# Three of the four quarters of the first modulations as fp32r pairs of high and low halves

## The chip, the cores and the metric

One core of one Trainium2 chip runs the whole program. The metric is the device time of one launch in microseconds. The engines work side by side, each through its own list of instructions in order, and wait for one another by semaphores: TensorE (PE in rows; its weight loads are PEld), VectorE (DVE), ScalarE (ACT), GpSimd (POOL) and SyncE (SP), whose list here is almost only DMA issues.

## The reference, cut to what matters

Two layers of a diffusion block over 512 latent and 256 context tokens of width 1024. What the change touches is the first sixth and second sixth of the adaLN modulations of layer 0 (shift and scale of the first norm), computed once for the latent and once for the context conditioning vector:

```python
silu_c = jax.nn.silu(c)
silu_ct = jax.nn.silu(c_ctx)
...
sh_a, sc_a, ga_a, sh_f, sc_f, ga_f = jnp.split((silu_c @ w_mod + b_mod)[:, None, :], 6, axis=-1)
tsh_a, tsc_a, tga_a, tsh_f, tsc_f, tga_f = jnp.split(silu_ct @ w_mod + b_mod, 6, axis=-1)
h = modulate(rms_norm(x, g_attn), sh_a, sc_a)
ht = modulate(rms_norm(xt, g_attn), tsh_a, tsc_a)
... = split_mixer_inputs(h @ w_in, qk_g)
... = split_mixer_inputs(ht @ w_in, qk_g)
```

`modulate(h, shift, scale)` is `h * (1 + scale) + shift`. All inputs are float32. Nothing of `h @ w_in` can begin before the shift and scale of its features are known.

## The kernel before

Activations lie features down, 128 features to a tile (`KT` = 8 tiles) and 768 tokens across (512 latent, 256 context). A product that must be near float32 is made of fp32r or f16 pairs: an operand is rounded to its high part, and the low part is the rest. `split` on GpSimd does it for a unit of weights (128 columns of `w_in`, in `raw_w`): one TENSOR_SCALAR writes the high half (L723) and one TENSOR_TENSOR subtracts it from the original for the low half (L726), into `split_w`. `dense_tile` (L958) then multiplies, for one feature tile k, weights high by activations high, weights low by activations high, and weights high by activations low: three products of 512 and 256 columns, six matmuls.

**The opening.** The first norm can't start without its modulations, and their weights, 8 MB for 2048 columns, come in four quarters, `mod_start[0..3]`: quarter i has the shift and the scale of feature tiles 2i and 2i+1. For each quarter:

1. TensorE, `first_modulations(i)` (L905): eight float32 matmuls, one for each input tile, with the two silu vectors (128x2) as weights and 512 columns moving, into the PSUM tile `small`.
2. ScalarE, `take_rows(i)` (L1385): the 2x512 result to `mod_rows`.
3. TensorE, `turn_first_modulations(i)` (L915): four transposes into `mod_ps`.
4. VectorE: `mod` = `mod_ps` plus bias (L1688), then `gain` from `mod` and the norm weights (L1692).
5. For each of the two tiles k: VectorE `scaled` = x_t times gain times inverse norm (L1773, its second tensor is `side` in PSUM), ScalarE `act` high = scaled plus shift, rounded (L1395, semaphore `h_hi`), VectorE `act` low = scaled plus shift minus high (L1757, function `lo`, semaphore `h_lo`). Each comes as two instructions, 512 and 256 columns.

TensorE takes the tiles in `dense_pair`: weight unit 0 at tile k and, `LAG` = 3 tiles later, unit 1. The next quarter's matmuls and transposes stand between tiles by hand:

```python
def in_tile(k):
    if l == 0 and k in (1, 3, 5):
        turn_first_modulations((k + 1) // 2)
    if l == 0 and k in (2, 4):
        first_modulations(1 + k // 2)
    pe.wait_ge(h_hi, 2 * l * KT + k + 1)
```

Quarter 1's eight matmuls come ahead of tile 0. GpSimd has nothing between the split of unit 1 and that of unit 2, which waits until unit 0's matmuls are done, since both use one slot of `split_w`. SyncE issues, in this order: tokens, mod_start 0 and 1, weight units 0 and 1, mod_start 2, small constants, mod_start 3. Everything behind the opening (units 2 to 15, attention, output projection, FFN, second layer) is the same in both kernels.

## Time and profile before

| | |
|---|---|
| median of 3 runs | 1706.69 us (1705.18 to 1708.16) |
| the profiled execution, its own time | 1705.99 us |
| its span | 1704.2 us |
| TensorE busy | 1632.2 us (96%) |
| VectorE, ScalarE, GpSimd busy | 1025.6, 745.2, 739.6 us |

The span is from the first to the last instruction; the time has 1.8 us more around it. Busy time of an engine says how much of the span it had an instruction in flight. The chain that ended last follows, back from the end, at each step what released the waiting instruction; "issue" is a step for which the profile shows no wait. A time in brackets behind a row of the timeline is what the engine idled before it, and for whom.

### The profile page before, as it was taken

Reading aid. Unit: us, or ns where it says so; the run is one execution under the profiler, and the core shown is the slowest. Engines: PE = TensorE matmul, PEld = TensorE weight load, DVE = VectorE, ACT = ScalarE, POOL = GpSimd, SP = SyncE. Lnnn points to the kernel's source line nnn. Section 1 sums busy time; section 2 is a strip of 40 time slices with the busy share of each in tenths; the row PEclk is TensorE's granted clock in tenths of the full one; section 3 lists DMA queues with packets and bytes.
Section 4 is the critical chain, followed back from the end, with each engine's and each line's share of the span. In section 5 each row is a group of like instructions: output and inputs, shape, how many; then the busy total and the mean of one; then the engine's idle time right before and its main releaser. Section 6 shows DMA issues by size and latency. Waiting matters only on the chain.

```text
span 1704.2 us, 29725 instructions
## 1 busy us (share of the span) xinstructions
PE 1632.2 (96%) x11685; PEld 1120.3 (66%) x11685; DVE 1025.6 (60%) x2075; ACT 745.2 (44%) x1367; POOL 739.6 (43%) x474
## 2 busy tenths in 40 slices
PE   7999989998999999999999999997998899999998
PEld 3688878977856656666666667886887544444444
DVE  3434498884479873788358855456995526326234
ACT  4222278884144341334313323225894455355342
POOL 1244335572614443344433343550403567567563
PEclk9999999999989999999999999998999899999999
DMA  9355453323045412353326232554103242243222
GB/s 325 58 133 138 118 150 98 94 63 88 26 123 161 137 56 93 99 164 120 113 75 225 79 69 53 135 135 114 28 6 101 62 136 87 75 136 96 66 87 87
DMA packets 317290, 179.24 MB, mean 105 GB/s; under 512 B 88527, under 2 KB 310495, under 8 KB 317151
## 3 DMA queue, kind: packets, MB, share of 16 engines
q1 hardware_dynamic: 284542, 143.63, 30.6%
q10 hardware_dynamic: 32608, 33.71, 6.2%
q8 instruction: 93, 1.52, 0.4%
q14 instruction: 47, 0.38, 0.1%
HBM read 158.97 MB, written 2.83 MB: 95 GB/s over the span
## 4 chain that ended last, share of the span: by engine, by line
PE 73%; DVE 15%; issue 5%; ACT 3%; DMA 2%; SPq 1%; POOL 1%; ACTq 0%; DVEq 0%; POOLq 0%
PE acc L958 60%; DVE mod_acc L2148 4%; DVE prob L1930 2%; DVE prob_t L1936 2%; PE small L905 2%; PE mod_ps L1058 1%; PE side L1143 1%; PE side L895 1%; ACT prob_t L1516 1%; PE acc L1126 1%; PE acc L1127 1%; DVE mod_acc L2146 1%; ACT prob L1494 1%; DMA tokens<-in_ctx 1%; PE mod_ps L1143 1%
## 5 line engine op out<-in xcount | busy, mean ns | idle before, releaser
L958 PE MATMUL acc<-act,pair_w 128*128 128x512 f16 x3168 | 580.2, 345 | 5.6 <-ACT act L1395 3.5
L958 PEld LDWEIGHTS acc<-act,pair_w 128*128 128x128 f16 x3168 | 309.5, 99 | 265.5 <-issue 10.6
L958 PE MATMUL acc<-act,split_w 128*128 128x512 f32 (+1 forms) x1920 | 378.6, 355 | 9.3 <-DVE act L2080 4.6
L958 PEld LDWEIGHTS acc<-act,split_w 128*128 128x128 f32 x1920 | 307.7, 189 | 63.6 <-DVE act L2080 6.8
L799 POOL TENSOR_SCALAR pair_raw<-pair_raw,weight_scale 128x1024 f32<-128x1024 f32 x88 | 109.6, 1246 | 324.9 <-ACT pair_w L1566 324.9
L958 PE MATMUL acc<-hidden,down_w 128*128 128x512 f16 (+1 forms) x1056 | 247.8, 343 | 1.6 <-DVE hidden L2114 0.8
L723 POOL TENSOR_SCALAR split_w<-raw_w 128x1024 fp32r<-128x1024 f32 x72 | 77.1, 1071 | 342.9 <-PE acc L958 231.0
L2148 DVE SCALAR_TENSOR_TENSOR mod_acc<-mod_chunk,silu_c,mod_acc 128x256 f32<-128x256 f32 x280 | 198.0, 751 | 4.0
L802 POOL TENSOR_TENSOR pair_w<-pair_raw,pair_w 128x1024 f16<-128x1024 f32 x88 | 192.4, 2187 | 7.3
L726 POOL TENSOR_TENSOR split_w<-raw_w,split_w 128x1024 fp32r<-128x1024 f32 x72 | 171.9, 2388 | 6.0
L2109 DVE SCALAR_TENSOR_TENSOR prod<-acc,prod_scale,silu_g 128x768 f32<-128x768 f32 (+1 forms) x44 | 38.9, 884 | 208.0 <-PE acc L958 199.0
L958 PEld LDWEIGHTS acc<-hidden,down_w 128*128 128x128 f16 x1056 | 100.5, 98 | 85.2 <-POOL down_w L818 2.8
L958 PE MATMUL acc<-hidden,down_low 128*128 128x512 f16 (+1 forms) x528 | 152.6, 343 | 0.0
L1635 ACT ACTIVATE hidden<-prod 128x768 f16<-128x768 f32 (+1 forms) x44 | 32.4, 736 | 238.4 <-DVE prod L2109 238.4
L1494 ACT ACTIVATE prob<-prob,stat 128x768 f32<-128x768 f32 (+5 forms) x160 | 121.7, 761 | 32.7 <-DVE prob L1930 25.8
L1930 DVE TENSOR_SCALAR_CACHE_REDUCE prob<-acc,score_scale 128x768 f32<-128x768 f32 (+4 forms) x128 | 102.7, 802 | 12.0 <-PE acc L1127 9.2
L1566 ACT ACTIVATE pair_w<-pair_raw,weight_scale 128x1024 f16<-128x1024 f32 x88 | 95.9, 1137 | 16.5 <-DVE weight_scale L2027 16.5
L1555 ACT ACTIVATE squares_out<-pair_raw 128x1024 bf16<-128x1024 f32 x88 | 92.4, 1050 | 7.5 <-DMA pair_raw<-in_w_up 3.5
L1784 DVE SCALAR_TENSOR_TENSOR x_t<-acc,down_gate,x_t 128x512 f32<-128x512 f32 x72 | 45.4, 658 | 80.4 <-PE acc L958 80.2
L1628 ACT ACTIVATE silu_g<-acc,weight_scale 128x768 f32<-128x768 f32 (+1 forms) x44 | 34.6, 786 | 132.9 <-PE acc L958 99.5
L1126 PE MATMUL acc<-ks,qs 128*128 128x256 f16 (+1 forms) x384 | 91.6, 270 | 0.0
L1127 PE MATMUL acc<-ks,qs 128*128 128x256 f16 (+1 forms) x384 | 89.3, 269 | 0.0
(229 smaller groups left out, 2462.8 us busy)
## 6 DMA issues: line engine op xcount, KB each, us to landing
mod_chunk<-in_w_mod ACTq DMA_DIRECT2D x28, 1024.0 KB, 5.2
pair_raw<-in_w_gate SPq DMA_DIRECT2D x44, 512.0 KB, 3.7
pair_raw<-in_w_up SPq DMA_DIRECT2D x44, 512.0 KB, 4.8
raw_w<-in_w_in SPq DMA_DIRECT2D x64, 256.0 KB, 3.8
raw_w<-in_w_mod SPq DMA_DIRECT2D x24, 512.0 KB, 4.0
raw_w<-in_w_down SPq DMA_DIRECT2D x20, 512.0 KB, 4.5
mod_start<-in_w_mod SPq DMA_DIRECT2D x8, 1024.0 KB, 11.0
ks<-q_split SPq DMA_DIRECT2D x64, 96.0 KB, 2.4
```

Of the source, the lines that this page charges most:

```text
L723: pool.tensor_scalar(split_w[slot][:, 0, 0:n, :], raw_w[slot][:, 0:n, :], 1.0, 0.0, ALU.mult, ALU.add).then_inc(hi_w, 1)
L726: pool.tensor_tensor(split_w[slot][:, 1, 0:n, :], raw_w[slot][:, 0:n, :], split_w[slot][:, 0, 0:n, :].bitcast(F32), ALU.subtract).then_inc ...
L799: pool.tensor_scalar(raw, raw, weight_scale[:, 1, 2 * f + s:2 * f + s + 1], 0.0, ALU.mult, ALU.add).then_inc(weight_mul, 1)
L802: pool.tensor_tensor(w[:, s, 1, :, :], raw, w[:, s, 0, :, :], ALU.subtract).then_inc(pair_ready, 1)
L958: mm = pe.matmul(acc[slot][:, a:b], own, moving[:, part == 1, k, a:b], start=(k == 0 and part == 0), stop=(k == n - 1 and part == 1))
L1126: pe.matmul(out_, q, ks[:, s["k"], 0, k0:k0 + size], start=True, stop=False)
L1127: mm = pe.matmul(out_, q, ks[:, s["k"], 1, k0:k0 + size], start=False, stop=not masks)
L1494: sc.activation(p, p, ACT.Exp, bias=stat[:, 1, i:i + 1], scale=-1.0, accum_out=stat[:, 2, i:i + 1]).then_inc(exps, 1)
L1555: sc.activation(squares_out[:, :], pair_raw[home(f)][:, s, :, :].rearrange("p k n -> p (k n)"), ACT.Square, accum_out=weight_sum[:, 2 * f ...
L1566: sc.activation(pair_w[home(f)][:, s, 0, :, :], pair_raw[home(f)][:, s, :, :], ACT.Copy, scale=weight_scale[:, 1, 2 * f + s:2 * f + s + 1] ...
L1930: ve.tensor_scalar(out_, src, minus, None, ALU.mult, ALU.min, accum_out=lowest).then_inc(scored, 1)
L2148: s = ve.scalar_tensor_tensor(**kw, in1=kw["out"], op0=ALU.mult, op1=ALU.add)
```

## The change

Quarter 0 stays as it is. Quarters 1 to 3 are taken as pairs. ScalarE rounds `mod_start[i]` to fp32r in four pieces of 128x1024 (`round_first`, into `mod_high`), and GpSimd, or VectorE for the first `LOW_BY_DVE[i]` pieces, subtracts them for the low halves (`split_first` and `low_first`, in place, as `mod_low`). TensorE runs eight fp32r matmuls on the high halves and eight on the low ones, with the four columns of `silu4` (high and low of both vectors) as weights, and the result has four rows. The transposes of these quarters become small matmuls with `fold`, which also adds the rows of the high and the low silu. TensorE's order in the first pair of units changes too: unit 1 follows unit 0 tile by tile, with no lag. SyncE loads weight unit 0 ahead of mod_start 1.

```diff
+LOW_BY_DVE = [0, 2, 0, 0]
...
             load_start(0)
+            load_in(0, 0)
             load_start(1)
-            load_in(0, 0)
             load_in(0, 1)
             load_start(2)
...
+                def split_first(i):
+
+                    pool.wait_ge(mod_start_in[i], 32)
+                    for p in range(LOW_BY_DVE[i], 4):
+                        pool.wait_ge(first_hi, 4 * (i - 1) + p + 1)
+                        pool.tensor_tensor(mod_low[i][:, 2 * p:2 * p + 2, :], mod_start[i][:, 2 * p:2 * p + 2, :],
+                                           high_at(i, 2 * p, 2).bitcast(F32), ALU.subtract).then_inc(first_lo_pool, 1)
+
                 for j in range(16):
                     split(u_in(l) + j, 8)
+                    if l == 0 and j == 1:
+                        for i in range(1, N_START):
+                            split_first(i)
...
+            def high_modulations(i):
+
+                pe.wait_ge(mod_rows_ready, i)
...
+                for k in range(KT):
+                    if k % 2 == 0:
+                        pe.wait_ge(first_hi, 4 * (i - 1) + k // 2 + 1)
+                    pe.matmul(small[0:4, :], silu4[:, k, :], high_at(i, k, 1).rearrange("p k n -> p (k n)"),
+                              start=(k == 0), stop=False)
+
+            def low_modulations(i):
+
+                for k in range(KT):
+                    if k == 0 and sum(LOW_BY_DVE[:i + 1]):
+                        pe.wait_ge(first_lo_dve, sum(LOW_BY_DVE[:i + 1]))
+                    if k == 2 * LOW_BY_DVE[i]:
+                        pe.wait_ge(first_lo_pool, 4 * i - sum(LOW_BY_DVE[:i + 1]))
+                    mm = pe.matmul(small[0:4, :], silu4[:, k, :], mod_low[i][:, k, :], start=False, stop=(k == KT - 1))
                 mm.then_inc(mod_start_done, 1)
...
+                def first_pair(r):
+
+                    for k in range(KT):
+                        in_tile(k)
+                        dense_tile(0, split_w[0], k, KT, act, TOK, in_tile_low)
+                        if k == 0:
+                            pe.wait_ge(split_ready, r + 2)
+                        if k % 2 and k < KT - 1:
+                            low_modulations((k + 1) // 2)
+                        dense_tile(1, split_w[1], k, KT, act, TOK)
+                        if k % 2 and k < KT - 1:
+                            turn_first_modulations((k + 1) // 2)
+                            if k < KT - 3:
+                                high_modulations((k + 3) // 2)
...
+            def round_first(i, pieces):
+                sc.wait_ge(mod_start_in[i], 32)
...
+                for p in pieces:
+                    sc.activation(high_at(i, 2 * p, 2), mod_start[i][:, 2 * p:2 * p + 2, :], ACT.Copy).then_inc(first_hi, 1)
...
-                    if nu == 0 and k % 2 == 0:
+                    if nu == 0 and k == 0:
+                        round_first(1, (0, 1))
+                        take_rows(0)
+                        round_first(1, (2, 3))
+                    elif nu == 0 and k % 2 == 0:
+                        if k < KT - 2:
+                            round_first(k // 2 + 1, range(4))
                         take_rows(k // 2)
...
+                def low_first(i):
+
+                    for p in range(LOW_BY_DVE[i]):
+                        ve.wait_ge(first_hi, 4 * (i - 1) + p + 1)
+                        ve.tensor_tensor(mod_low[i][:, 2 * p:2 * p + 2, :], mod_start[i][:, 2 * p:2 * p + 2, :],
+                                         high_at(i, 2 * p, 2).bitcast(F32), ALU.subtract).then_inc(first_lo_dve, 1)
+
...
+                    if nu == 0 and k % 2 and k < KT - 1:
+                        low_first((k + 1) // 2)
```

GpSimd's list at the start, before. The numbers behind a tile's name tell its buffers apart (`split_w_52` and `_53` are the slots of units 0 and 1, and then of units 2 and 3).

```order
L723 TENSOR_SCALAR split_w_52<-raw_w_50 128x1024
L726 TENSOR_TENSOR split_w_52<-raw_w_50,split_w_52 128x1024
L723 TENSOR_SCALAR split_w_53<-raw_w_51 128x1024
L726 TENSOR_TENSOR split_w_53<-raw_w_51,split_w_53 128x1024
L723 TENSOR_SCALAR split_w_52<-raw_w_50 128x1024
L726 TENSOR_TENSOR split_w_52<-raw_w_50,split_w_52 128x1024
```

The same place now (L733 and L736 are the split, L756 is `split_first`):

```order
L733 TENSOR_SCALAR split_w_52<-raw_w_50 128x1024
L736 TENSOR_TENSOR split_w_52<-raw_w_50,split_w_52 128x1024
L733 TENSOR_SCALAR split_w_53<-raw_w_51 128x1024
L736 TENSOR_TENSOR split_w_53<-raw_w_51,split_w_53 128x1024
L756 TENSOR_TENSOR mod_low_124<-mod_start_121,mod_high_128 128x1024 x2
L756 TENSOR_TENSOR mod_low_125<-mod_start_122,mod_high_129 128x1024 x2
L756 TENSOR_TENSOR mod_low_125<-mod_start_122,mod_high_130 128x1024 x2
L756 TENSOR_TENSOR mod_low_126<-mod_start_123,mod_high_131 128x1024 x2
L756 TENSOR_TENSOR mod_low_126<-mod_start_123,mod_high_132 128x1024 x2
L733 TENSOR_SCALAR split_w_52<-raw_w_50 128x1024
L736 TENSOR_TENSOR split_w_52<-raw_w_50,split_w_52 128x1024
```

Ten two-input subtractions now stand between the split of unit 1 and that of unit 2. VectorE's list from the first modulations of quarter 0 to those of quarter 1, before:

```order
L1688 TENSOR_TENSOR mod<-mod_ps,vecs 128x2x4
L1692 SCALAR_TENSOR_TENSOR gain<-mod,vecs 128x4
L1773 SCALAR_TENSOR_TENSOR scaled_137<-x_t,gain,side 128x512
L1773 SCALAR_TENSOR_TENSOR scaled_137<-x_t,gain,side 128x256
L1773 SCALAR_TENSOR_TENSOR scaled_138<-x_t,gain,side 128x512
L1773 SCALAR_TENSOR_TENSOR scaled_138<-x_t,gain,side 128x256
L1757 SCALAR_TENSOR_TENSOR act<-scaled_137,mod,act 128x512
L1757 SCALAR_TENSOR_TENSOR act<-scaled_137,mod,act 128x256
L1757 SCALAR_TENSOR_TENSOR act<-scaled_138,mod,act 128x512
L1757 SCALAR_TENSOR_TENSOR act<-scaled_138,mod,act 128x256
L1688 TENSOR_TENSOR mod<-mod_ps,vecs 128x2x4
```

And now, from the last `scaled` of quarter 0 on (L1832 is `lo`, L1841 is `low_first`):

```order
L1855 SCALAR_TENSOR_TENSOR scaled_147<-x_t,gain,side 128x256
L1832 SCALAR_TENSOR_TENSOR act<-scaled_146,mod,act 128x512
L1832 SCALAR_TENSOR_TENSOR act<-scaled_146,mod,act 128x256
L1841 TENSOR_TENSOR mod_low_124<-mod_start_121,mod_high_127 128x1024 x2
L1832 SCALAR_TENSOR_TENSOR act<-scaled_147,mod,act 128x512
L1832 SCALAR_TENSOR_TENSOR act<-scaled_147,mod,act 128x256
L1763 TENSOR_TENSOR mod<-mod_ps,vecs 128x2x4
```

Two subtractions of 1024 columns stand between the low half of tile 0 and that of tile 1; in quarters 2 and 3 VectorE's order is as before. TensorE's list in quarter 1 is now the following (L1002 is `dense_tile`, `_52` for unit 0 and `_53` for unit 1; L946 the low halves, L936 the high ones, L957 the turning):

```order
L1002 MATMUL acc<-act,split_w_52 128x512
L1002 MATMUL acc<-act,split_w_52 128x256
L946 MATMUL small<-mod_low_124,silu_87 4x512 x8
L1002 MATMUL acc<-act,split_w_53 128x512
L1002 MATMUL acc<-act,split_w_53 128x256
L1002 MATMUL acc<-act,split_w_53 128x512
L1002 MATMUL acc<-act,split_w_53 128x256
L1002 MATMUL acc<-act,split_w_53 128x512
L1002 MATMUL acc<-act,split_w_53 128x256
L957 MATMUL mod_ps<-fold,mod_rows_151 128x2 x4
L936 MATMUL small<-mod_high_129,silu_87 4x512 x4
L936 MATMUL small<-mod_high_130,silu_87 4x512 x4
```

The low halves of quarter 1 come behind tile 1 of unit 0, so the turning that gives tiles 2 and 3 their modulations comes behind that tile's low half as well.

## Rows read from the trace of the kernel before

**Rows 1.** The page: span, and TensorE's busy time, share and instructions.

```profile
span 1704.2 us, 29725 instructions
...
PE 1632.2 (96%) x11685; PEld 1120.3 (66%) x11685; DVE 1025.6 (60%) x2075; ACT 745.2 (44%) x1367; POOL 739.6 (43%) x474
```

**Rows 2.** Chain of waits, opening: start us, us, engine, tile, line, count.

```profile
29.78 6.96 PE small L905 x16
...
37.99 0.34 PE mod_ps L915 x4
...
47.78 0.34 PE mod_ps L915 x4
...
57.38 2.28 PE acc L958 x12
59.66 0.35 PE mod_ps L915 x4
...
63.96 6.93 PE acc L958 x38
```

**Rows 3.** Groups by form, 0 to 130 us: busy us, mean ns, idle before.

```profile
L726 POOL TENSOR_TENSOR split_w<-raw_w,split_w 128x1024 fp32r<-128x1024 f32 x9 | 21.5, 2389 | 0.7
...
L1331 ACT ACTIVATE squares_tok<-tokens 128x1024 bf16<-128x1024 f32 x6 | 6.3, 1054 | 3.0 <-DMA tokens<-in_x 2.9
...
L1757 DVE SCALAR_TENSOR_TENSOR act<-scaled,mod,act 128x512 fp32r<-128x512 f32 x8 | 6.0, 749 | 0.6
...
L1757 DVE SCALAR_TENSOR_TENSOR act<-scaled,mod,act 128x256 fp32r<-128x256 f32 x8 | 3.8, 480 | 0.0
```

**Rows 4.** Timeline, VectorE and GpSimd near 30 us: start us, us, engine, line.

```profile
30.12 0.25 DVE L1692 SCALAR_TENSOR_TENSOR gain<-mod,vecs 128x4 f32<-128x4 f32 x1
...
30.40 2.19 DVE L1773 SCALAR_TENSOR_TENSOR scaled<-x_t,gain,side 128x512 f32<-128x512 f32 x4
30.44 2.36 POOL L726 TENSOR_TENSOR split_w<-raw_w,split_w 128x1024 fp32r<-128x1024 f32 x1
```

**Rows 5.** Timeline, VectorE beside GpSimd near 91 and 888 us.

```profile
91.12 2.40 POOL L726 TENSOR_TENSOR split_w<-raw_w,split_w 128x1024 fp32r<-128x1024 f32 x1
...
92.74 1.07 DVE L1842 SCALAR_TENSOR_TENSOR q_raw<-raw_q,vecs,inv 128x256 f32<-128x256 f32 x1 [1.10 <-DMA inv<-inv_rows]
...
887.84 2.18 POOL L802 TENSOR_TENSOR pair_w<-pair_raw,pair_w 128x1024 f16<-128x1024 f32 x1
888.05 2.24 DVE L2148 SCALAR_TENSOR_TENSOR mod_acc<-mod_chunk,silu_c,mod_acc 128x256 f32<-128x256 f32 x1
...
889.99 1.29 POOL L799 TENSOR_SCALAR pair_raw<-pair_raw,weight_scale 128x1024 f32<-128x1024 f32 x1
890.33 1.22 DVE L2148 SCALAR_TENSOR_TENSOR mod_acc<-mod_chunk,silu_c,mod_acc 128x256 f32<-128x256 f32 x1
```

**Rows 6.** Queue of SyncE by tile: mod_start issued 9 to 15, raw_w 22 to 25.

```profile
L512 SPq DMA_DIRECT2D mod_start<-in_w_mod x2: 2701/3152/3602, 8.7 to 12.4; - x2
...
DMA to landing us min/median/max: 11.0/11.5/11.9
...
L521 SPq DMA_DIRECT2D raw_w<-in_w_in x2: 1126/1818/2511, 20.6 to 23.2; - x2
...
DMA to landing us min/median/max: 4.5/5.4/6.3
```

**Rows 7.** TensorE's timeline at 468, then busy time by stretch (PEclk is the clock).

```profile
468.66 1.50 PE L936 MATMUL side<-ones,sq 128*128 128x1 f32 x12 [1.56 <-ACT sq L1368]
...
476.00:480.00 4.00, 4.00 (x15) 1.88 (x14) 3.93 (x9) 1.58 (x4) 0.00 (x0) 0.50 0.00 1
...
213.00:217.00 4.00, 4.00 (x26) 3.42 (x25) 3.51 (x8) 3.82 (x8) 0.00 (x0) 0.50 0.86 242
```

**Rows 8.** Timeline near the end of the first two weight units.

```profile
66.85 1.05 POOL L723 TENSOR_SCALAR split_w<-raw_w 128x1024 fp32r<-128x1024 f32 x1 [34.05 <-PE acc L958]
...
71.30 8.65 PE L958 MATMUL acc<-act,split_w 128*128 128x512 f32 x48
```

More of the change, by code:

```diff
@@ L327, in trunk @@
             mod_start[i] = place(f"mod_start{i}", [P, 8, 4 * P], F32, where)
+        mod_low = [None] + [place(f"mod_low{i}", [P, 8, 4 * P], F32R, where)
+                            for i, where in ((1, b0 + 24576), (2, b0 + 47104), (3, b0))]
+        mod_high = [place(f"mod_high{i}", [P, 4, 4 * P], F32R, where)
+                    for i, where in enumerate((a0 + 30720, a0 + 38912, b0 + 16384, b0 + 65536 + 6144, b0 + 24576, b0 + 32768))]
         c0 = at[0]
@@ L339, in trunk @@
         scaled_ffn = [place(f"scaled_ffn{i}", [P, TOK], F32, c0 + 8192 + i * 3072) for i in range(2)]
-        mod_rows = place("mod_rows", [2, MOD_FIRST * P], F32, c0 + 2048)
+        mod_rows = [place(f"mod_rows{i}", [4, 4 * P], F32, c0 + 2048 + 2048 * i) for i in range(2)]
         mod_chunk = [place(f"mod_chunk{i}", [P, 8, 2 * P], F32, b0 + 49152 + i * 8192) for i in range(2)]
@@ L386, in trunk @@
         mod_start_done, mod_rows_ready = sem("mod_start_done"), sem("mod_rows_ready")
+        first_hi, first_lo_dve, first_lo_pool = sem("first_hi"), sem("first_lo_dve"), sem("first_lo_pool")
         mod_chunk_in = [sem(f"mod_chunk_in{i}") for i in range(2)]
@@ L474, in freed, with high_at @@
             return ring[r - 2][0] + 1 if r >= 2 else None
+        def high_at(i, k0, n):
+            return mod_high[2 * (i - 1) + k0 // 4][:, k0 % 4:k0 % 4 + n, :]
         def width(l):
@@ L897, in modulation, with first_modulations @@
                 mm.then_inc(unit_done, 1)
-            def first_modulations(i):
-                pe.wait_ge(mod_start_in[i], 32)
-                if i:
-                    pe.wait_ge(mod_rows_ready, i)
+            def first_modulations():
+                pe.wait_ge(mod_start_in[0], 32)
                 for k in range(KT):
-                    mm = pe.matmul(small[0:2, :], silu_c[:, k::KT], mod_start[i][:, k, :],
+                    mm = pe.matmul(small[0:2, :], silu_c[:, k::KT], mod_start[0][:, k, :],
                                    start=(k == 0), stop=(k == KT - 1))
+                mm.then_inc(mod_start_done, 1)
+            def high_modulations(i):
+                pe.wait_ge(mod_rows_ready, i)
+                if i == 1:
+                    pe.wait_ge(silu_split, 2)
+                for k in range(KT):
[10 more added lines that the diff above has]
+                    mm = pe.matmul(small[0:4, :], silu4[:, k, :], mod_low[i][:, k, :], start=False, stop=(k == KT - 1))
                 mm.then_inc(mod_start_done, 1)
@@ L914, in turn_first_modulations @@
                 for a in range(2 * START_TILES):
-                    mm = pe.transpose(mod_ps[:, 2 * a:2 * a + 2], mod_rows[:, 512 * i + P * a:512 * i + P * a + P], ident[0:2, 0:2])
+                    row = mod_rows[i % 2][:, P * a:P * a + P]
+                    if i:
+                        mm = pe.matmul(mod_ps[:, 2 * a:2 * a + 2], row, fold[:, :], start=True, stop=True)
+                    else:
+                        mm = pe.transpose(mod_ps[:, 2 * a:2 * a + 2], row[0:2, :], ident[0:2, 0:2])
                 mm.then_inc(mod_first, 1)
@@ L1004, in _ @@
                     pe.wait_ge(vec_ready, 1)
-                    first_modulations(0)
+                    first_modulations()
                 else:
@@ L1010, in _ @@
                     turn_first_modulations(0)
-                    first_modulations(1)
+                    high_modulations(1)
                 def in_tile(k):
-                    if l == 0 and k in (1, 3, 5):
-                        turn_first_modulations((k + 1) // 2)
-                    if l == 0 and k in (2, 4):
-                        first_modulations(1 + k // 2)
                     pe.wait_ge(h_hi, 2 * l * KT + k + 1)
@@ L1083, in _ @@
                             pe.wait_ge(resid, 32 * l)
-                        if j == 0:
+                        if j == 0 and l:
                             pe.wait_ge(split_ready, ring_of[u] + 2)
-                            dense_pair(split_w, act, TOK, in_tile, in_tile_low, 1 if l else LAG)
+                            dense_pair(split_w, act, TOK, in_tile, in_tile_low, 1)
+                        elif j == 0:
+                            first_pair(ring_of[u])
                         elif j >= 2:
@@ L1384, in take_rows @@
                 sc.wait_ge(mod_start_done, i + 1)
-                sc.activation(mod_rows[:, 512 * i:512 * i + 512], small[0:2, :], ACT.Copy).then_inc(mod_rows_ready, 1)
+                if i >= 2:
+                    sc.wait_ge(mod_first, i - 1)
+                n = 4 if i else 2
+                sc.activation(mod_rows[i % 2][0:n, :], small[0:n, :], ACT.Copy).then_inc(mod_rows_ready, 1)
+            def round_first(i, pieces):
+                sc.wait_ge(mod_start_in[i], 32)
+                if i == 2:
+                    sc.wait_ge(xt_ps, KT)
+                elif i == 3:
+                    sc.wait_ge(mod_start_done, 2)
+                for p in pieces:
+                    sc.activation(high_at(i, 2 * p, 2), mod_start[i][:, 2 * p:2 * p + 2, :], ACT.Copy).then_inc(first_hi, 1)
             def shifted(nu, l, w):
```

## The prediction, made before the changed kernel ran

> **What bounds the kernel now.** I read the page first: TensorE is busy for 1632.2 of 1704.2 us [rows 1], so whatever lengthens or shortens the time until TensorE can run freely shifts the end by as much. Then the chain of waits over the opening, the only stretch that the change touches [rows 2]. It is TensorE's almost throughout: one quarter's eight float32 matmuls take 6.96 us. The ends of the four turnings give marks: T0 = 29.8 (where the row of quarter 1's matmuls begins), T1 = 38.3, T2 = 48.1, T3 = 60.0. At T3 the chain leaves TensorE for VectorE and ScalarE and is back at 63.96 with 38 matmuls in 6.93 us. Unit 2 starts at 71.3 [rows 8]. That is the mark that counts: behind it both kernels issue the same work. Last I read how VectorE and GpSimd share time, since the change gives GpSimd ten instructions just where it idled 34 us [rows 8].
>
> **What is removed.** 24 float32 matmuls, 3 x 6.96 = 20.9 us of TensorE.
>
> **What is added on TensorE.** 48 matmuls of 512 columns. Twelve matmuls of a tile pair (six of 512 and six of 256 columns) take 2.28 us [rows 2], so one of 512 costs 0.25 at most; start to start inside such a run I take 0.23. Sixteen a quarter: 3.7 us, 11.0 in all. TensorE's work falls by 9.9 us; the fold matmuls cost what the transposes did (0.34 for four).
> The Trainium skill's page "TensorE: Matmul & The Clock Gate" (section "Back-to-back issue gap") gives about 131 ns for a matmul of 512 columns in a sustained stream with weight loads; by that, sixteen would take 2.1 us and TensorE would save 14.6 us in all. The row with its 2.28 us for 4608 columns speaks against it.
>
> **What is added elsewhere.** ScalarE: twelve roundings of 128x1024; its squares of that shape take 1.05 us [rows 3], so 4.2 a quarter. GpSimd: ten subtractions of the form of L726, 2.36 to 2.39 us each [rows 3, 4], 23.7 us. VectorE: two of 1024 columns. Its row of 512 columns is 0.75 and that of 256 is 0.48 [rows 3], so 1.05 ns a column and 0.2 fixed: 1.3 each, 1.1 of it streaming.
>
> **The loads.** mod_start 1 landed at 12.4 + 11.0 = 23.4, weight unit 1 at 23.2 + 4.5 = 27.7 [rows 6]. Weight unit 0 (two loads, which landed about 1.2 us apart) now goes ahead: mod_start 1 lands near 25.9, unit 1 as before. ScalarE rounds two pieces from 25.9 to 28.0 and copies the rows of quarter 0 by 28.6, ahead of TensorE's turning at 29.4. So T0 stays 29.8. Each us that the load is later than 26.7 would delay T0 by one.
>
> **VectorE against GpSimd.** This decides. A multiply-add of 256 columns with two SBUF inputs takes 0.48 us alone. Next to GpSimd it took 2.24 (888.05, beside a subtraction that ran until 890.02) and then 1.22 (890.33, beside a GpSimd row until 891.28); both end 0.27 us after the GpSimd row beside them, which is 256 columns of streaming [rows 5]. So it waited for the whole of that GpSimd instruction. And GpSimd's next began streaming only behind it: 1.29 for the form that takes 1.1 to 1.2. With GpSimd's list full, the two alternate, one instruction each. The same beside L726, the very form that is added: 1.07 at 92.74 [rows 5]. Near 30 us the four `scaled`, whose second tensor is in PSUM, ran through in 2.19 us, while `gain` (four columns, two SBUF inputs) took 0.25 and ended only with GpSimd's pass [rows 4]. So `scaled` and `mod` are free of it; `gain`, both instructions of each `lo`, and `low_first` are not.
> The Trainium skill's page "SBUF — State Buffer" (section "SBUF: two separate sides") says it as a rule: GpSimd and a VectorE operation with two SBUF inputs contend for one shared pair of ports, held exclusively for the whole instruction. The trace agrees (0.48 against 2.24).
>
> **The walk.** Unit 1 lands at 27.7, so its high half runs 27.8 to 28.8 and its low half to 31.2; `gain` of quarter 0 now meets the latter and ends at 31.3 (before: 30.4). `scaled` of tiles 0 and 1 take 2.2, and the high half of tile 0 is there at 33.6 (before 32.7). GpSimd goes straight on from 31.2: two pieces of quarter 1, then four of quarter 2, whose high halves ScalarE gives from 35.7 to 38.9, in time. VectorE has six instructions that contend, before tile 1 is complete: `lo`(0) in two, two of `low_first`, `lo`(1) in two. Their streaming parts are 0.53 + 0.27 + 1.07 + 1.07 + 0.53 + 0.27 = 3.7 us. Between the six lie five GpSimd turns of 2.36, less about 0.1 each of start that is hidden: 11.3. So `lo`(1) ends at 33.7 + 3.7 + 11.3 = 48.7. TensorE, done with the high parts of tile 1 at 39, idles ten us. Then two matmuls of the tile 0.35, eight low ones 1.85, tile 1 of unit 1 1.05, turning 0.4: **T1 = 52.4, 14.1 later** than 38.3.
> T1 to T2: GpSimd is out of pieces (quarter 3's are rounded only behind `act`(3), 4.9 us after T1). VectorE 0.4, `scaled` 1.15, `act` 1.15, `lo` 1.15, last part of tile 2 0.35, tile 2 of unit 1 and tile 3 of unit 0 2.1, eight low matmuls 1.85, tile 3 of unit 1 and turning 1.4: 9.5, before 9.8: -0.3.
> T2 to T3: quarter 3's four subtractions run from 4.9 to about 14.3 us after T1, so `gain` of quarter 2 waits for one (+2.1): 11.5, before 11.9: -0.4.
> T3 to unit 2: 2.75 until tile 6, its six matmuls with the wait for `lo` 1.5, tile 6 of unit 1 1.05, tile 7 1.05 (unit 0 done: T3 + 6.4). Unit 2's split (1.05 + 2.4) can only start there. Before, three lagging tiles of unit 1 covered it; that cover is gone, so TensorE waits for the split: T3 + 9.8, before 11.3: -1.5.
> Sum 14.1 - 0.3 - 0.4 - 1.5 = **+11.9 us**.
>
> **The clock.** At 468 TensorE idled 1.56 us and then ran one-column matmuls; from 470 on its granted clock was at 0.5 (1.2 GHz), also through 4 us of full work from 476 [rows 7]; in another stretch, 213 to 217, it was 0.5 with TensorE busy throughout. An idle time of ten us ahead of T1, and shorter ones before it, will cost such a stretch: some 7 us of work at half speed in place of 3.5. I take **+3.5**; bounds are 0 (it rises during waits) and 7 (a second fall in the 3 us wait ahead of tile 4).
>
> Total +15.4. On the profiled execution's 1705.99 (span 1704.2 and 1.8 around it; the median of the three runs, 1706.69, is 0.7 more) that is 1721.4; I say **1721.5 us**.
>
> **The rivals.** A difference under 0.2% (3.4 us) is about what can't be told from none.
> (a) *The subtractions and `lo` don't disturb each other*: `lo` would have to run beside GpSimd as `scaled` does. `lo` itself was never beside a running GpSimd for more than 0.1 us (749 and 480 ns, [rows 3]), so nothing shows it directly. The walk then gives T1 = 40.7, T2 = 50.1, T3 = 59.6, unit 2 at 69.4, 1.9 earlier: 1704.1. TensorE's 9.9 us go into its waits for `h_hi` and `h_lo` (about 1.0 + 0.5 a quarter), the low piece on VectorE (1.3), the lost lag and the exposed split. 8%.
> (b) *The other side*: TensorE stays the bound of the opening, the 9.9 us all arrive, 1696. Mechanism: the high matmuls of the next quarter and the tiles fill every wait. It decides once unit 2 starts before 67.9, so that under 6.5 of the 9.9 us are lost; against it, even walk (a) loses 8.0, and unit 2's split alone needs 3.5 behind unit 0. 4%, together with the gains of (a) that come out a little over 3.4.
> (c) *Half of the alternation*: VectorE's pairs (512 and 256 columns, no wait between them) keep the ports, so only four turns come between. Turns saved ahead of T1: two of 2.36, +7.2 without the clock, +9 with some of it: 1714. 12%.
> (d) *Full alternation, clock near full or falling once*: the forecast, 1718 to 1723.5. 52%.
> (e) *The clock falls twice, or the load of mod_start 1 comes late*: 1724 to 1728. 24%.
>
> **The numbers.** (c), (d) and (e) are slower, 88%. Range for 8 in 10: it leaves out (b), (a) and the far end of (e): 1711 to 1727. Faster by over 0.2%: 4%; within: 8%; slower: 88%.
>
> **What would show it.** In the changed kernel's timeline from 33 to 49 us, rows of L1832 and L1841 should be 1.5 to 3.4 us long in place of 0.75, 0.48 and 1.3, each ending right behind a row of L756. TensorE should idle near 39 to 49, T1 should be at 52 to 55, and unit 2 at 83 to 89. From T1 to T2 L1832 should be 0.75 and 0.48 again. GpSimd's split of unit 2 should start with the end of unit 0's matmuls and TensorE wait for it. The granted clock should show a stretch at 0.5 around T1. I am wrong if L1832 keeps its 0.75 beside running subtractions, or if GpSimd's rows, not VectorE's, take the delay.

## The result, and the profile after

The changed kernel took 1725.6 us (median of 4 runs) against 1707.2 us for the kernel before: a ratio of **1.0111, 95% interval 1.0097 to 1.0126**. Run again beside another set of runs of the kernel before it took 1724.2 against 1706.3, ratio 1.0096 [1.0078, 1.0114]. So it is 1% slower, 16.4 to 18.9 us; forecast were 14.8 to 15.4. The ratios are the record's own and not quotients of the medians shown. The profiled execution of the first measurement was disturbed (4239.82 us; the other three took 1724.4 to 1726.5, median 1724.8), so the profile shown here is that of the second one. Its execution took 1726.6 us, the longest of its four (from 1720.0 on). The page:

```profile
span 1724.8 us, 29782 instructions
...
PE 1631.9 (95%) x11697; PEld 1124.8 (65%) x11697; DVE 1042.4 (60%) x2077; ACT 756.4 (44%) x1379; POOL 765.1 (44%) x484
```

TensorE's busy time is what it was (1632.2 before, [rows 1]). 9.9 us of matmuls less don't show in it: at half clock a matmul is busy for nearly twice as long (the eight low ones below 3.41 us at 0.50, 1.85 at 1.00), and the fold matmuls are dearer than was thought, as below. GpSimd has 25.5 us more.

The chain of waits of the changed kernel over the opening: start us, us, engine, tile, line, count. It answers to [rows 2].

```profile
28.87 0.35 PE mod_ps L959 x4
...
33.16 5.32 DVE act L1832 x2
38.48 6.61 DVE mod_low L1841 x2
45.09 3.15 DVE act L1832 x2
...
49.29 3.41 PE small L946 x8
52.70 1.46 PE acc L1002 x6
54.16 0.99 PE mod_ps L957 x8
...
59.11 2.72 PE acc L1002 x14
...
64.74 0.99 PE mod_ps L957 x8
...
65.96 1.20 DVE gain L1767
...
70.71 4.19 PE acc L1002 x14
...
77.80 0.99 PE mod_ps L957 x8
...
81.56 6.14 PE acc L1002 x18
...
87.86 1.05 POOL split_w L733
...
88.99 2.36 POOL split_w L736
...
91.39 1.67 PE acc L1002 x8
```

The chain that was TensorE's is now VectorE's for 15 us on end, from 33.16 to 48.24. The marks: T0 = 29.2, T1 = 55.15, T2 = 65.7, T3 = 78.8, unit 2 at 91.39. It was at 71.30 [rows 8], so 20.1 us went in here. From unit 2 to the end of the span both kernels take about 1633 us (1704.2 - 71.3 and 1724.8 - 91.4), so nothing came or went behind the opening.

Timeline of VectorE and GpSimd in the stretch in which VectorE holds the chain (separate answers; a row of x2 is two instructions back to back):

```profile
33.16 2.82 DVE L1832 SCALAR_TENSOR_TENSOR act<-scaled,mod,act 128x512 fp32r<-128x512 f32 x1
...
35.91 2.57 DVE L1832 SCALAR_TENSOR_TENSOR act<-scaled,mod,act 128x256 fp32r<-128x256 f32 x1
...
38.41 3.39 DVE L1841 TENSOR_TENSOR mod_low<-mod_start,mod_high 128x1024 fp32r<-128x1024 f32 x1
...
35.40 5.32 POOL L756 TENSOR_TENSOR mod_low<-mod_start,mod_high 128x1024 fp32r<-128x1024 f32 x2
...
40.67 6.61 POOL L756 TENSOR_TENSOR mod_low<-mod_start,mod_high 128x1024 fp32r<-128x1024 f32 x2
```

`lo` of 512 columns was 0.75 us [rows 3] and is 2.82, that of 256 columns was 0.48 and is 2.57. The difference is 2.1 both times, whatever its size: not a slower stream but one turn of GpSimd. And GpSimd's own row grows from 2.39 to 3.3 (6.61 for two) where VectorE's part between is 1024 columns. In the next quarter, where GpSimd has no piece, four instructions of L1832 take 2.21 us together:

```profile
57.91 2.21 DVE L1832 SCALAR_TENSOR_TENSOR act<-scaled,mod,act 128x512 fp32r<-128x512 f32 x4
```

Windows of the changed kernel: stretch, us, then busy time and instructions of PE, PEld, DVE, ACT, POOL, then the granted clock.

```profile
36.00:40.00 4.00, 1.47 (x5) 1.28 (x6) 4.00 (x2) 1.97 (x3) 4.00 (x2) 0.55 1.09 376
...
44.00:48.00 4.00, 0.00 (x0) 0.00 (x0) 4.00 (x3) 0.00 (x0) 3.28 (x2) 0.83 0.88 79
48.00:52.00 4.00, 3.71 (x9) 1.49 (x10) 0.23 (x1) 0.00 (x0) 0.00 (x0) 0.50 1.13 108
...
80.00:84.00 4.00, 2.44 (x7) 2.13 (x8) 3.61 (x7) 2.17 (x4) 0.00 (x0) 0.60 0.01 2
84.00:88.00 4.00, 4.00 (x15) 3.39 (x14) 0.27 (x1) 0.00 (x0) 0.14 (x1) 0.55 0.00 0
```

TensorE idles from 44 to 48 and then works at 0.50, 1.2 GHz. The clock falls again behind the waits of the later quarters. It had already fallen once before, at 0.55 from 36 to 40, since TensorE waits twice ahead of T1: 4.31 us for the low half of tile 0 and, from 42.74 to 48.28, 5.54 us for that of tile 1. Its row between the two waits:

```profile
38.53 4.21 PE L1002 MATMUL acc<-act,split_w 128*128 128x512 f32 x12 [4.31 <-DVE act L1832]
```

Twelve such matmuls take 2.3 us in the kernel before. Here this costs nothing, because VectorE holds the chain.

### The profile page after: what moved, and what is told of

The parts are those of the page before. It is cut to its first block, busy times and chain, and to the rows that moved or that the text cites. A ratio compares the mean times of both kernels' runs of the same rounds, so it can differ in the third digit from the quotient of the medians.

```text
span 4238.0 us, 29782 instructions
## 1 busy us (share of the span) xinstructions
PE 4202.3 (99%) x11697; PEld 2207.6 (52%) x11697; DVE 1024.6 (24%) x2077; ACT 761.4 (18%) x1379; POOL 757.4 (18%) x484
## 4 chain that ended last, share of the span: by engine, by line
PE 99%; DVE 1%; ACT 0%; DMA 0%; issue 0%; SPq 0%; DVEq 0%; ACTq 0%
PE acc L1002 77%; PE side L1200 3%; PE acc L1184 2%; PE acc L1183 2%; PE mod_ps L1200 2%; PE mod_ps L1113 2%; PE small L1217 1%; PE small L1218 1%; PE small L1219 1%; PE side L916 1%; PE small L1300 1%; PE small L924 0%; PE side L990 0%; PE small L946 0%; PE side L1251 0%; PE acc L1187 0%
## 5 line engine op out<-in xcount | busy, mean ns | idle before, releaser
L1002 PE MATMUL acc<-act,pair_w 128*128 128x512 f16 x3168 | 1573.7, 735 | 3.5 <-ACT act L1470 3.5
L1002 PEld LDWEIGHTS acc<-act,pair_w 128*128 128x128 f16 x3168 | 554.8, 176 | 995.0 <-issue 866.5
L1002 PE MATMUL acc<-act,split_w 128*128 128x512 f32 (+1 forms) x1920 | 940.9, 718 | 8.8 <-ACT act L1470 4.6
L1002 PEld LDWEIGHTS acc<-act,split_w 128*128 128x128 f32 x1920 | 647.5, 364 | 259.6 <-issue 243.5
L1002 PE MATMUL acc<-hidden,down_w 128*128 128x512 f16 (+1 forms) x1056 | 604.4, 733 | 0.0
L1002 PEld LDWEIGHTS acc<-hidden,down_w 128*128 128x128 f16 x1056 | 180.6, 174 | 319.6 <-issue 275.1
L1002 PE MATMUL acc<-hidden,down_low 128*128 128x512 f16 (+1 forms) x528 | 345.4, 735 | 0.0
L733 POOL TENSOR_SCALAR split_w<-raw_w 128x1024 fp32r<-128x1024 f32 x72 | 75.2, 1045 | 1224.5 <-PE acc L1002 927.8
L1184 PE MATMUL acc<-ks,qs 128*128 128x256 f16 (+1 forms) x384 | 188.5, 509 | 0.0
L1183 PE MATMUL acc<-ks,qs 128*128 128x256 f16 (+1 forms) x384 | 186.7, 493 | 0.0
L1002 PEld LDWEIGHTS acc<-hidden,down_low 128*128 128x128 f16 x528 | 93.0, 176 | 169.2 <-issue 147.8
L736 POOL TENSOR_TENSOR split_w<-raw_w,split_w 128x1024 fp32r<-128x1024 f32 x72 | 170.0, 2361 | 6.0
L1200 PE MATMUL side<-ident,prob 128*128 128x128 f32 x467 | 169.9, 536 | 0.0
L1217 PE MATMUL small<-v,prob_t 128*128 128x64 f16 x696 | 166.0, 291 | 0.0
L1218 PE MATMUL small<-v,prob_t 128*128 128x64 f16 x696 | 161.6, 288 | 0.0
```

The source lines that it names most:

```text
L733: pool.tensor_scalar(split_w[slot][:, 0, 0:n, :], raw_w[slot][:, 0:n, :], 1.0, 0.0, ALU.mult, ALU.add).then_inc(hi_w, 1)
L736: pool.tensor_tensor(split_w[slot][:, 1, 0:n, :], raw_w[slot][:, 0:n, :], split_w[slot][:, 0, 0:n, :].bitcast(F32), ALU.subtract).then_inc ...
L1002: mm = pe.matmul(acc[slot][:, a:b], own, moving[:, part == 1, k, a:b], start=(k == 0 and part == 0), stop=(k == n - 1 and part == 1))
L1183: pe.matmul(out_, q, ks[:, s["k"], 0, k0:k0 + size], start=True, stop=False)
L1184: mm = pe.matmul(out_, q, ks[:, s["k"], 1, k0:k0 + size], start=False, stop=not masks)
L1200: mm = pe.transpose(turned_at[BANK_AT["p", c] % 3][:, t - a:t - a + P], prob[g % 3][:, 1 + t:1 + t + P], ident[:, :])
```

## The experiments

The theory: two-input instructions of GpSimd and VectorE take turns, one instruction each, and this makes the low halves late. The rivals: the subtractions cost only as work in a chain, whoever does them; TensorE's changed order and lost lag are the cause; the transfers or the mere activity of GpSimd are.

T0 falls anywhere from 28.8 to 31.2 us in the profiles that follow. Two of the kernels are those of the kernel before up to T0 and have it at 28.81 and 30.88. So where marks of two runs are compared, their distance from T0 counts: a table of it stands behind the last experiment.

**The changed kernel again** (no edit).

> The changed kernel, nothing edited, for an undisturbed profile. Full alternation of VectorE and GpSimd: 1724 to 1726 us, rows of L1832 and L1841 from 33 to 49 us take 1.5 to 3.4 us each and end right behind a row of L756, TensorE idles some ten us near 39 to 49, T1 at 52 to 55, unit 2 at 83 to 90, a stretch of the granted clock at 0.5 around T1. Rival, that the loss is in TensorE's order (no lag, split of unit 2 exposed): L1832 keeps 0.75 and 0.48 us, and the loss shows ahead of unit 2 alone.

1.0096 [1.0078, 1.0114]; this is the profile above. The rows of L1832 and L1841 are as expected. T1 (55.15) and unit 2 (91.39) come a little later than expected, and TensorE has two waits of 4.3 and 5.5 us in place of one of ten. T0 is no later in this profile than before, so the changed order of the loads delays nothing in it.

**Without the subtractions.** The low matmuls read the high halves, and the low halves are never made; so the product with them is another one, while TensorE and ScalarE have the same work.

```diff
-                        for i in range(1, N_START):
-                            split_first(i)
...
-                        low_first((k + 1) // 2)
...
-                    mm = pe.matmul(small[0:4, :], silu4[:, k, :], mod_low[i][:, k, :], ...)
+                    mm = pe.matmul(small[0:4, :], silu4[:, k, :], high_at(i, k, 1)..., ...)
```

> The changed kernel without its twelve subtractions: the low matmuls read the high halves again, so that this kernel computes something else in the first modulations. ScalarE's roundings, TensorE's 48 matmuls and their order stay. If the subtractions cost the time by the ports, L1832 falls back to 0.75 and 0.48 us, T1 comes at 39 to 40, unit 2 at 68 to 69, and the time is 1703 to 1706 us. If TensorE's order or the later load is what costs, it stays within 3 us of 1725.

1708.9 us, 1.0009 [0.9999, 1.0018], some 3 us above what was expected. The slowdown goes with the subtractions: 1.0096 - 1.0009 is 0.87%, 14.8 us. But the 9.9 us that TensorE saves don't come either. Its timeline (at the row's end the idle time before it, and for whom):

```profile
39.59 1.05 PE L950 MATMUL mod_ps<-fold,mod_rows 4*128 4x2 f32 x8
...
64.55 6.92 PE L995 MATMUL acc<-act,split_w 128*128 128x512 f32 x24 [2.79 <-ACT act L1463]
...
74.13 2.26 PE L995 MATMUL acc<-act,split_w 128*128 128x512 f32 x11
```

T1 is 40.6 (the forecast's undisturbed walk had 40.7), but a quarter takes 10.56 us, from one turning to the next; TensorE waits at each for the activations, and unit 2 comes at 74.13, not 69.4. That is 45.3 us behind T0, where the kernel before has 41.6.

**The subtractions alone, in the kernel before.** Ten GpSimd subtractions of the same shape behind the split of unit 1, on data that nobody needs, so that nothing waits for them.

```diff
+                    if l == 0 and j == 1:
...
+                        for i in range(10):
...
+                            pool.tensor_tensor(spare[0][:, :, :], x_t[:, 0:2, 0:512], x_t[:, 3:5, 0:512],
+                                               ALU.subtract).then_inc(spare_done, 1)
```

> The kernel before, with ten GpSimd subtractions of 128x1024 put behind the split of unit 1, which nobody waits for; they read x_t and write a spare tile. Exclusive ports: from 33 to about 60 us each contending VectorE instruction waits for a GpSimd one, T2 comes 3 us later and T3 some 5, the time is 1711 to 1714 us. If VectorE and GpSimd don't disturb each other: 1706 to 1708 us, no change.

1715.3 us, 1.0051 [1.0036, 1.0066]: 8.7 us for work that no instruction waits for, and a us more than the 1711 to 1714 expected. From its chain:

```profile
31.74 10.50 DVE act L1768 x4
...
42.35 2.13 DVE gain L1703
44.50 1.15 DVE scaled L1784 x2
...
46.83 8.52 DVE act L1768 x4
```

Four `lo` take 10.50 us in place of 2.21, `gain` 2.13 in place of 0.17, and two `scaled`, whose second tensor is in PSUM, 1.15 as ever. A part of the 8.7 us is the clock: TensorE waits 3.39 us for a low half, and its next eight float32 matmuls take 8.59 us in place of 7.03, at a granted clock of 0.50 from 44 to 46.

**The same place, GpSimd only writing.** 24 memsets of 128x1024 in place of the ten subtractions.

```diff
+                        for i in range(24):
...
+                            pool.memset(spare[:, :, :], 1.0).then_inc(spare_done, 1)
```

> The kernel before with 24 GpSimd memsets of 128x1024 behind the split of unit 1, which read nothing and which nobody waits for. If what contends is reading SBUF, VectorE's L-rows of the low halves keep 0.75 and 0.48 us beside them and the time stays at 1706 to 1708 us; if any GpSimd instruction holds the ports, they are lengthened as beside the subtractions and the time is over 1709.

1706.2 us, 1.0002 [0.9991, 1.0013]. GpSimd and VectorE in its timeline:

```profile
31.70 24.16 POOL L751 MEMSET spare<- 128x1024 f32 x24
...
34.14 2.21 DVE L1766 SCALAR_TENSOR_TENSOR act<-scaled,mod,act 128x512 fp32r<-128x512 f32 x4
```

GpSimd is busy without a gap, and `lo` keeps its time. So it isn't GpSimd's activity, nor its writing to SBUF.

**The kernel before without its lag.**

```diff
-                            dense_pair(split_w, act, TOK, in_tile, in_tile_low, 1 if l else LAG)
+                            dense_pair(split_w, act, TOK, in_tile, in_tile_low, 1 if l else 0)
```

> The kernel before, with one number changed: the first pair of weight units without a lag (0 in place of 3), as in the changed kernel. The split of unit 2 is then exposed: T1 39.4, T2 51.4, T3 63.4, unit 2 at 73.4, 2 us later than before: 1708 to 1710 us. If the lag was worth nothing: 1706 to 1708. If the order is the main loss of the change: over 1715.

1709.9 us, 1.0021 [1.0010, 1.0032]: the lag alone is worth 3.6 us. In the profile unit 2 comes 43.8 us behind T0 in place of 41.6, 2.2 us later, where 2 were expected. Without it the chain goes through the split of unit 2:

```profile
68.27 2.74 PE acc L958 x14
...
71.16 1.05 POOL split_w L723
...
72.29 2.36 POOL split_w L726
```

**All twelve subtractions on VectorE.**

```diff
-LOW_BY_DVE = [0, 2, 0, 0]
+LOW_BY_DVE = [0, 4, 4, 4]
```

> The changed kernel with LOW_BY_DVE = [0, 4, 4, 4]: all twelve subtractions on VectorE, none on GpSimd. If GpSimd's instructions are the price by the ports, each of L1841 takes 1.2 us, undisturbed, and L1832 0.75 and 0.48; VectorE's 4.8 us a quarter lie on the chain ahead of lo of the odd tile: T1 at 45, T2 58, T3 72, unit 2 at 83 to 86, 1717 to 1722 us. If VectorE and GpSimd don't disturb each other, this must be slower than the changed kernel: over 1726.

1720.9 us, 1.0082 [1.0066, 1.0097], as expected. Nothing alternates any more (two `lo` take 1.15 us again), and little is won; the interval overlaps with that of the changed kernel, [1.0078, 1.0114]. Its chain has VectorE's four pieces whole, in every quarter, ahead of the low half that TensorE waits for.

```profile
50.91 4.54 DVE mod_low L1841 x4
...
57.57 3.41 PE small L946 x8
```

The pieces are 3 x 4.54 = 13.6 us of chain. Between this ratio and the one without subtractions lie 12.4 us, but that the two are so near is in part chance: the half clock adds to it (the low matmuls of the three quarters take 3.10, 3.41 and 3.41 us in place of 1.85), and TensorE's work beside the pieces takes off. It is also why unit 2 comes at 91.7 and not at 83 to 86. So the rival "they cost as work in the chain" holds where they stand there: taking turns is how the change loses its time, not the only way to lose it.

**Another order.** Lag restored, the sixteen matmuls of a quarter in a row, the loads as in the kernel before, all pieces on VectorE, those of quarter 1 ahead of the modulations of quarter 0. Of the edit:

```diff
+                if nu == 0:
+                    low_first(1)
                 ve.wait_ge(inv_spread, 2 * nu + 1)
...
-                            first_pair(ring_of[u])
+                            dense_pair(split_w, act, TOK, in_tile, in_tile_low, 1 if l else LAG)
```

> The changed kernel rearranged: the loads and TensorE's tile order with lag 3 of the kernel before, high and low matmuls of a quarter together where its float32 matmuls stood, all subtractions on VectorE (those of quarter 1 ahead of its wait for the inverse norm, those of quarters 2 and 3 ahead of lo of the even tile), quarter rows copied ahead of the next roundings. If the ports and the chain behind lo are the whole loss, the fp32r pairs pay here: T1 35 to 36, T2 45 to 47, T3 56 to 58, unit 2 at 67 to 69, 1702 to 1704.5 us, faster than the kernel before by 2 to 4 us. If fp32r pairs cost more than they save in themselves: 1707 or more.

1707.6 us, 1.0007 [0.9994, 1.0020]: a miss, 1702 to 1704.5 were expected. Its timeline shows that the early pieces met GpSimd's splits of the weight units:

```profile
24.56 8.46 DVE L1824 TENSOR_TENSOR mod_low<-mod_start,mod_high 128x1024 fp32r<-128x1024 f32 x4 [0.75 <-ACT mod_high L1456]
...
33.14 2.14 DVE L1767 SCALAR_TENSOR_TENSOR gain<-mod,vecs 128x4 f32<-128x4 f32 x1
...
26.77 3.19 POOL L736 TENSOR_TENSOR split_w<-raw_w,split_w 128x1024 fp32r<-128x1024 f32 x1
29.94 2.02 POOL L733 TENSOR_SCALAR split_w<-raw_w 128x1024 fp32r<-128x1024 f32 x1
```

`gain` ends at 35.3, five us late. The split's first half (L733, one input) took 2.02 beside a piece, in place of 1.05: it takes turns too. Two more losses stand in this timeline. Behind a wait of 3.64 us TensorE works at 0.50 from 40 to 44 (the fold matmuls take 1.86 us in place of 1.05), and in quarter 3 three of the four pairs of low matmuls wait 0.35 to 0.51 us for their piece. What each of the losses costs was not tried by itself.

**The clock.** The changed kernel, with matmuls into an unused part of PSUM while TensorE waits for the low halves of tiles 0 and 1.

```diff
                 def in_tile_low(k):
+                    if l == 0 and k < 2:
+                        fill((30, 50)[k])
                     pe.wait_ge(h_lo, 2 * l * KT + k + 1)
```

> The changed kernel, with 30 matmuls of 256 columns into an unused part of PSUM while TensorE waits for the low half of tile 0, and 50 while it waits for that of tile 1, so that it is hardly idle from 34 to 48 us. If the half clock around the turning of quarter 1 comes from that idling and has a price, the eight low matmuls take 1.85 us in place of 3.41, the pieces of tile 1 next to them some 1.0 less in all, the turning of quarter 1 ends near 52.7 in place of 55.2, and unit 2 starts 2.5 us earlier: a ratio to the kernel before of 1.0080 to 1.0090 in place of 1.0096 to 1.0111, some 1720 to 1721.5 us. If the clock has no part in it, 1723.5 to 1725, or later where the filler overshoots its waits.

```profile
48.29 0.52 PE L1002 MATMUL acc<-act,split_w 128*128 128x512 f32 x2
48.64 2.02 PE L946 MATMUL small<-mod_low,silu 128*4 128x512 f32 x8
...
51.64 1.05 PE L957 MATMUL mod_ps<-fold,mod_rows 4*128 4x2 f32 x8
```

In this timeline the granted clock stays at 1.00 from 32 to 68 us, and from the last low half of tile 1 to the end of the turning it is 4.3 us (48.29 to 52.6) in place of 6.9 (48.28 to 55.15): 2.6 us, as expected. The time, 1721.0 us, has the ratio 1.0093 [1.0078, 1.0108], which can't be told from 1.0096 or surely from 1.0111. The profile shows the step; the timing doesn't resolve it. Nor is the time of this run a clean price of the clock. Its turns fell otherwise: the four pieces of quarter 2 start only at 37.92, VectorE meets three turns and not five, the low half of tile 1 is there at 46.77, and the filler overshoots it by some 1.5 us. Behind 68 us the clock falls here too (0.63 from 68 to 72).

**The fold matmuls.** Without subtractions, and the first two rows transposed in place of the fold, so that the products with the low half of silu are left out too.

```diff
-                    if i:
-                        mm = pe.matmul(mod_ps[:, 2 * a:2 * a + 2], row, fold[:, :], start=True, stop=True)
```

> As the run without subtractions, and the fold matmuls of quarters 1 to 3 are transposes of the first two rows again (so the products with the low half of silu are left out too). If the fold matmuls cost 1.0 a quarter where the transposes cost 0.35, each quarter is 0.65 us shorter and unit 2 starts 2.0 us earlier than without subtractions alone (72.2 in place of 74.1): 1704.5 to 1707. If the records only look longer, no difference: 1707 to 1709.

```profile
40.65 0.40 PE L950 MATMUL mod_ps<-ident,mod_rows 2*128 2x2 f32 x4
...
50.58 0.41 PE L950 MATMUL mod_ps<-ident,mod_rows 2*128 2x2 f32 x4
```

Start to start, turning 1 to turning 2 is 9.93 us, with the fold it is 10.56: 0.63 a quarter. The time, 1707.5 us, is 1.0011 [1.0000, 1.0022] against 1.0009, which is the case of no difference (1707 to 1709): two us that the profile shows and the timing doesn't; its intervals are as wide as that.

**What the scheme could give.** Without subtractions, and with the lag and all sixteen matmuls in a row (the order of the reordered run above, minus `low_first` and with weight unit 0 loaded ahead of mod_start 1).

> What the scheme could give at best: no subtractions (the low matmuls read the high halves), unit 1 three tiles behind unit 0 as in the kernel before, and all sixteen matmuls of a quarter in a row. The lag alone measured 1.0021, and the run without subtractions 1.0009. If the waits for the activations absorb what TensorE saves, whatever the order, the lag gives its 2 to 4 us back at most and the time is 1702 to 1706. If TensorE is the bound of the opening again, its saving of 9.9 us less 2.0 for the fold matmuls arrives: 1697 to 1700.

1697.3 us, **0.9959 [0.9945, 0.9972]**, the second of the two cases: TensorE is the bound again and the saving arrives. Its timeline has no idle time of TensorE from 29.61 to 54.3, and unit 2 comes 33.7 us behind T0. That is 7.9 less than in the kernel before, just what 9.9 us less 2.0 for the fold matmuls give. So what the run without subtractions lost lay in TensorE's order: 8.5 us by the ratios (1.0009 to 0.9959), 11.6 in the two profiles (45.3 to 33.7 behind T0). Of the latter some 2.5 are the half clock at the end of that run (24 matmuls in 6.92 us; the kernel before has 24 in 4.46). The lag and the sixteen matmuls in a row came together here and were not told apart. The reordered run has the same order with its twelve subtractions on VectorE: from 1.0007 to 0.9959 it is 8.2 us that they cost there.

**A version that beats both.** Nothing is left out of it. Quarters 1 and 3 as pairs, quarter 2 in float32, the lag restored. Of each pair quarter VectorE subtracts three pieces where it idled and GpSimd one, released by `gain` and so beside `scaled`; the split of unit 1 waits for the gain of quarter 1.

```diff
+LOW_BY_DVE = [0, 3, 0, 3]
...
+                    pool.wait_ge(gain_ready, i)
                     for p in range(LOW_BY_DVE[i], 4):
...
                 for j in range(16):
+                    if l == 0 and j == 1:
+                        pool.wait_ge(gain_ready, 2)
                     split(u_in(l) + j, 8)
```

> A version that computes the reference and keeps subtractions away from VectorE's contending instructions. Quarters 1 and 3 as pairs, quarter 2 in float32 as before; unit 1 three tiles behind unit 0 as before. Of each pair quarter VectorE subtracts three pieces where it idles (ahead of the modulations of quarter 0, and of those of quarter 2), and GpSimd one, which starts behind gain, so beside scaled, that it does not disturb. The split of weight unit 1 moves behind the gain of quarter 1. TensorE has 2 x (6.96 - 3.7) = 6.5 us less to do and 1.3 more for two quarters of fold matmuls, so 5.2 less. If the alternation is avoided and TensorE stays the bound as in the run with the lag and without subtractions (0.9959 for three quarters), two thirds of that gain: 1700 to 1702.5, ratio 0.9965 to 0.998. If one contention is left (one GpSimd turn of 2.4 us on the chain, or T0 late again), 1703 to 1707.

1702.0 us, **0.998 [0.9969, 0.999]**, at the upper edge of what was expected and 3.6 us (0.2%) faster than the kernel before. Its timeline, VectorE, then GpSimd:

```profile
25.55 3.50 DVE L1834 TENSOR_TENSOR mod_low<-mod_start,mod_high 128x1024 fp32r<-128x1024 f32 x3 [1.42 <-ACT mod_high L1466]
...
31.31 0.16 DVE L1777 SCALAR_TENSOR_TENSOR gain<-mod,vecs 128x4 f32<-128x4 f32 x1
31.51 2.19 DVE L1869 SCALAR_TENSOR_TENSOR scaled<-x_t,gain,side 128x512 f32<-128x512 f32 x4
33.84 2.21 DVE L1851 SCALAR_TENSOR_TENSOR act<-scaled,mod,act 128x512 fp32r<-128x512 f32 x4
...
39.56 3.22 DVE L1851 SCALAR_TENSOR_TENSOR act<-scaled,mod,act 128x512 fp32r<-128x512 f32 x4
...
31.61 2.42 POOL L757 TENSOR_TENSOR mod_low<-mod_start,mod_high 128x1024 fp32r<-128x1024 f32 x1 [8.96 <-DVE gain L1777]
...
38.42 2.36 POOL L736 TENSOR_TENSOR split_w<-raw_w,split_w 128x1024 fp32r<-128x1024 f32 x1
```

`gain` 0.16, `scaled` 2.19, `lo` 2.21, GpSimd's piece 2.42: in quarter 0 neither delays the other. It isn't free of the contention everywhere: in quarter 1 the four `lo` meet the split of unit 1 and take 3.22 us, and in quarter 3 TensorE waits 0.84 us for GpSimd's piece. From T0 to unit 2 it is 37.4 us (30.90 to 68.30) where the kernel before has 41.6.

**All profiles side by side.** T0 and unit 2 are the starts of TensorE's rows behind the first turning and of the third weight unit, as its timeline has them.

| run | T0 | unit 2 | from T0 to unit 2, us | ratio of the times |
|---|---|---|---|---|
| kernel before | 29.71 | 71.30 | 41.6 | 1 |
| changed kernel | 29.14 | 91.39 | 62.2 | 1.0096 |
| without subtractions | 28.85 | 74.13 | 45.3 | 1.0009 |
| before, ten spare subtractions | 28.81 | 77.95 | 49.1 | 1.0051 |
| before, memsets | 30.23 | 71.81 | 41.6 | 1.0002 |
| before, no lag | 30.88 | 74.69 | 43.8 | 1.0021 |
| all subtractions on VectorE | 31.20 | 91.72 | 60.5 | 1.0082 |
| reordered | 30.24 | 73.93 | 43.7 | 1.0007 |
| changed, filler | 31.12 | 87.89 | 56.8 | 1.0093 |
| no subtractions, transposes | 30.97 | 72.78 | 41.8 | 1.0011 |
| no subtractions, lag | 29.61 | 63.34 | 33.7 | 0.9959 |
| two quarters as pairs | 30.90 | 68.30 | 37.4 | 0.9980 |

One profile is one execution, and a ratio comes from all of a kernel's; what lies behind unit 2 also differs from one execution to another, so the two columns agree only to some 5 us.

## Why the prediction was right, and where its terms were off

- **Which way, and why: right.** The forecast was full alternation. The rows of L1832 and L1841 are 2.57 to 3.39 us as foretold (1.5 to 3.4), all but the last. In time: ten subtractions alone cost 8.7 us (1.0051), taking all away leaves 1.0009, and GpSimd busy with writing alone costs nothing. Against half alternation (c): the 256 columns of `lo`(0) wait for a turn of their own right behind the 512 (2.57 us). Against no disturbance (a): the same rows.
- **The walk to `lo`(1): right to half a us.** 48.7 forecast, 48.24 measured, from a T0 that came 0.6 earlier. The count of turns, five, is right, but their places are not, and that they make up for each other is luck. The forecast had none ahead of the first of the six instructions and one between each two. Measured, the first (33.16) came just behind the start of a piece and waited for all of it, and GpSimd's last piece ended at 47.28, so that the sixth, the 256 columns of `lo`(1), had no turn and took some 0.5 us.
- **One wait of ten us ahead of T1: not so.** TensorE was to idle from 39 to 49. It waited 4.31 us to 38.53 and 5.54 us to 48.28, since VectorE's late `lo`(0) held it up first. For T1 it is the same, because VectorE holds the chain throughout.
- **The fold matmuls: mis-sized.** "The fold matmuls cost what the transposes did (0.34 for four)": the rows say 0.99 a quarter; the run with transposes gives 0.63 a quarter in the profile, 1.9 us over three.
- **The clock: mis-sized.** +3.5 for one fall, bounds 0 to 7. The rows show three stretches: behind `lo`(1) 2.6 us (measured with the filler); 1.5 in the third quarter (4.19 for the 14 matmuls that take 2.72 at full clock); and behind T3 about 2.6 (unit 0 ends 6.3 us after tile 6 begins where 3.65 was reckoned; the clock there is 0.60 and 0.55, and how much of it is the clock was not tried by itself). Together 6.7, near the upper bound. That the clock falls more than once was case (e), given 24%, which the profiled execution fits and the medians of the timed runs (1724 and 1726) do too, on the edge to the forecast's own case (d), given 52%.
- **The sum for the profiled execution:** +15.4 forecast; fold +2.0, clock +3.2, T0 -0.6, `gain` of quarter 2 -1.1, the walk's small pieces the rest, +1.2; +20.1 measured. The medians are 2.7 and 4.1 us above the 1721.5. Unit 2 at 91.39 lies outside the 83 to 89 that were given as a sign, T1 at 55.15 just outside 52 to 55.
- **Quarter by quarter:** T1 to T2 is 10.55 for 9.5, of it 0.65 the fold. T2 to T3 is 13.1 for 11.5: fold and clock; `gain` of quarter 2 met one piece as said, but took 1.20 in place of 0.17, so it lost 1.0 and not 2.1. The exposed split of unit 2 is there as said (87.86 to 91.35).
- **Rival (a)'s price was wrong.** It said that without disturbance the time would be 1704.1. The run without subtractions gave 1708.9: its quarters take 10.56 and not 9.4, and the clock falls once at the end (0.50 from 64 to 68).
- **Seen, but too small:** that the order, not the pairs, eats TensorE's saving. Rival (a) names the lost lag and the exposed split, but beside waits for the activations and with no price of their own. With the lag, the sixteen matmuls in a row and no subtractions 8.5 us come back. Rival (b) was given 4% as a forecast for this change, rightly, since the change doesn't have that order. Its outcome, TensorE as the bound of the opening, is what the run with the lag and without subtractions showed, though there by another order than the one (b) spoke of.

The Trainium skill's rule of the shared pair of ports, held for a whole instruction (page "SBUF — State Buffer", section "SBUF: two separate sides"), agrees with the turns of 2.1 us here.

## What to carry to other kernels

Before giving GpSimd two-input work, list which VectorE instructions with two SBUF inputs fall beside it, and add one whole GpSimd instruction for each: here five such turns, of some 2.1 us each, cost more than the 7.9 us that the matmuls save. If the work is needed, release it by a semaphore so that it runs beside VectorE instructions whose second input is in PSUM, or where VectorE idles. And when work is taken off the bounding engine, keep the lag that covers its waits: here the lag was worth 3.6 us in the kernel before and, together with the order of the matmuls, 8.5 in the lighter one.
